# An encoder layer on one core: the 22 stores of the down product's activation forms are issued by GpSimd instead of ScalarE

## The reference

```
h = rmsnorm(x, ffn_norm_g)
gate, up = h @ w_gate_up                     # 512 x 2048 by 2048 x 11264
x = x + (silu(gate) * up) @ w_down           # 512 x 5632 by 5632 x 2048
```

## Time and profile before

| what | value |
|---|---|
| median of 3 runs | 2136.73 us (2135.73 to 2136.99) |
| profiled execution | 2136.44 us, its span in the trace 2134.7 us |
| PE | 2113.3 us busy, 99% of the span |
| DVE | 1526.2 us, 71% |
| ACT | 944.6 us, 44% |
| POOL | 174.2 us, 8% |
| granted TensorE clock | 0.998 of full speed |
| DMA | 376.31 MB, 176 GB/s over the span |

### The profile page before, as it was taken

The page is one execution under the profiler, slowest core; times in us unless marked ns, Lnnn a source line. Parts: engine busy times, 40 slices in busy tenths (PEclk is TensorE's granted clock), DMA queues, the critical chain, the costliest instruction groups (busy, mean ns, idle before and its releaser), DMA issues. The chain is left out here.

```text
span 2134.7 us, 27909 instructions
## 1 busy us (share of the span) xinstructions
PE 2113.3 (99%) x10404; PEld 1845.4 (86%) x10404; DVE 1526.2 (71%) x2108; ACT 944.6 (44%) x1281; POOL 174.2 (8%) x354
## 2 busy tenths in 40 slices
PE   8999999999999999999999999999999999999998
PEld 8999999999998888888888888888888777887876
DVE  4444444444455435888888987987978998999999
ACT  5333333333343335444444444544445554544533
POOL 0322222222221000000000000000000000000000
PEclk9999999999999999999999999999999999999999
DMA  6232333232243344666666666676677877868766
GB/s 185 76 99 79 93 85 92 79 98 79 84 128 128 119 134 132 198 218 200 219 212 211 208 219 212 204 233 204 198 235 232 269 256 246 263 208 269 260 186 203
DMA packets 258924, 376.31 MB, mean 176 GB/s; under 512 B 15842, under 2 KB 114180, under 8 KB 258324
## 3 DMA queue, kind: packets, MB, share of 16 engines
q1 hardware_dynamic: 255456, 354.90, 52.8%
q10 hardware_dynamic: 3380, 20.21, 2.5%
HBM read 346.45 MB, written 28.61 MB: 176 GB/s over the span
## 5 line engine op out<-in xcount | busy, mean ns | idle before, releaser
L1391 DVE TENSOR_TENSOR f_lo<-f_raw,f_hi 128x1536 fp32r<-128x1536 f32 (+1 forms) x230 | 454.4, 1980 | 46.9 <-ACT f_hi L1020 31.4
L564 PE MATMUL gemm<-w_hi,act_t 128*128 128x384 f32 (+2 forms) x1280 | 450.7, 352 | 2.3 <-DVE w_lo L1207 2.3
L565 PE MATMUL gemm<-w_lo,act_t 128*128 128x384 f32 (+2 forms) x1280 | 443.9, 347 | 0.0
L566 PE MATMUL gemm<-w_hi,act_t 128*128 128x384 f32 (+2 forms) x1280 | 443.9, 347 | 0.0
L765 PE MATMUL gemm<-f_hi,a_form 128*128 128x512 f32 x1056 | 411.2, 389 | 0.0
L767 PE MATMUL gemm<-f_hi,a_form 128*128 128x512 f32 x1056 | 411.1, 389 | 0.0
L766 PE MATMUL gemm<-f_lo,a_form 128*128 128x512 f32 x1056 | 410.8, 389 | 0.0
L765 PE MATMUL aux<-f_hi,a_form 128*128 128x512 f32 x792 | 313.2, 395 | 6.7 <-DVE f_lo L1391 5.1
L1207 DVE TENSOR_TENSOR w_lo<-w_raw,w_hi 128x768 fp32r<-128x768 f32 (+1 forms) x160 | 160.7, 1008 | 208.5 <-ACT w_hi L862 208.5
L766 PE MATMUL aux<-f_lo,a_form 128*128 128x512 f32 x792 | 308.5, 390 | 0.0
L767 PE MATMUL aux<-f_hi,a_form 128*128 128x512 f32 x792 | 308.5, 390 | 0.0
(11 more groups left out here) (184 smaller groups left out, 2227.5 us busy)
## 6 DMA issues: line engine op xcount, KB each, us to landing
f_raw<-in_ffn_w_gate_up SPq DMA_DIRECT2D x264, 512.0 KB, 4.2
f_raw<-in_ffn_w_down SPq DMA_DIRECT2D x132, 512.0 KB, 4.8
w_raw<-in_fox_w_in SPq DMA_DIRECT2D x192, 256.0 KB, 3.3
f_raw<-in_ffn_w_gate_up SPq DMA_DIRECT2D x88, 256.0 KB, 4.0
w_raw<-in_fox_w_out SPq DMA_DIRECT2D x16, 1024.0 KB, 5.1
f_raw<-in_ffn_w_down SPq DMA_DIRECT2D x44, 256.0 KB, 4.9
a_raw<-forms_scratch SPq DMA_DIRECT2D x22, 512.0 KB, 6.6
forms_scratch<-fa_a ACTq DMA_DIRECT2D x11, 896.0 KB, 6.3
```

Of the source, the lines that this page charges most:

```text
L564: mm(out, a_hi, b_hi, start=first, stop=False)
L565: mm(out, a_hi, b_lo, start=False, stop=False)
L566: return mm(out, a_lo, b_hi, start=False, stop=last)
L1391: v.tensor_tensor(f_lo[:, n % 4, 0:3 + g], f_raw[:, n % 4, 0:3 + g], f32(f_hi[:, n % 3, 0:3 + g]), ALU.subtract).then_inc(f_lo_done, 1)
```

## The change

The function `store_forms` and its two calls are gone from ACT's program. GpSimd issues the same 22 stores in the same order, each when DVE has signalled the forms of its step, right behind the norm factors and ahead of its two last adds.

```diff
@@ gpsimd
             g.tensor_scalar(rms_neg[:], rms_x[:], -1.0, None, ALU.mult).then_inc(rms2_done, 1)
+
+            for step in range(NSTEP):
+                pool.wait_ge(form_done, 8 + step + 1)
+                pool.dma_start(dram_forms[step], (fa_a, fa_b)[step % 2][:, 0:7])\
+                    .then_inc(forms_stored[step % 2], 16)
@@ scalar
-            def store_forms(r, i):
-                step = 2 * (r - 1) + i
-                act.wait_ge(form_done, 8 + step + 1)
-                act.dma_start(dram_forms[step], (fa_a, fa_b)[i][:, 0:7]).then_inc(forms_stored[i], 16)
-
@@ scalar, first pass
                     if j == 4 and hidden:
                         hidden_forms(r, 1)
-                    if j == 4 and hidden:
-                        store_forms(r, 0)
                 else:
-                    if j == 3 and hidden:
-                        store_forms(r, 1)
```

## The result

The changed kernel takes 2151.5 us (2150.16 to 2154.68, 4 runs) against 2136.86 us for the one before on the same chip: ratio 1.0071, 95% interval 1.0059 to 1.0083. It is 14.6 us slower, outside the range, with the sign and the place that stood in the text as the first rival, at 2143.9 us. The profiled execution took 2151.18 us, its span is 2149.2 us.

What follows compares the result with a forecast made beforehand. TensorE, busy 2113.3 of 2134.7 us, was taken to bound the kernel. 0 (issues) - 2.2 (second pass) + 3.3 (first pass) = +1.1 us on 2136.44 gave 2137.5 us, range 2132.8 to 2143.5.

Steps and rivals of the forecast that it cites:

- the first rival: Slower: fa_b's store shares engines with the second pass's first load every round, 0.7 us each; 2143.9 us, chance 0.26.
- What bounds it: TensorE bounds the kernel; in the SwiGLU half it waits 6.0 us in 10 waits for VectorE's low parts of weights.
- Issues on ScalarE worth nothing: Taking 22 store issues (7 us in all) off ScalarE frees nothing TensorE waits for: value 0.
- The gain in the second pass: Without fa_b's store there, TensorE's waits in rounds 4, 10 and 11 go: -2.2 us, ends 0 and -6.0.
- The limit of 6.4 us: Latest landing after issue of the second pass's first load that costs TensorE nothing, the same in every round.
- where the store stands beside the load: First pass's end: fa_b's store arrives 0.2 to 0.7 us after the load's second half's issue and stands behind it.
- The order of arrival: Transfers run in the order they arrive, read from fa_a's store moving no packet until 932.7 behind earlier loads.
- the price: Delay of the second pass's first load: 0.3 us in 11 rounds, 3.3 us; upper end 7.7 and about 2 more.
- The second, faster: Rival: stores stand behind loads and the first pass hides them; -2.2 to -6.0 us, 2131.9 us, chance 0.10.
- The third, a slow start on GpSimd: Rival: a GpSimd start over 8.3 us makes ScalarE wait for fa_a's memory; at 10 us 2155 us, chance 0.04.

Runs made afterwards that it cites:

- e3: Kernel before, with only the stores of fa_a moved to GpSimd, those of fa_b left on ScalarE at their old place: 2137.36 us, ratio 0.9993.
- f4: Changed kernel, with GpSimd's store of fa_b held until the sums of the second pass's last unit are done: 2132.58 us, ratio 0.9982.
- f2: Kernel before, with ScalarE's store of fa_b two units later in the second pass (j = 5 in place of 3): 2134.45 us, ratio 0.9987.
- g1: Changed kernel, with one unused GpSimd operation of about a microsecond ahead of each store of fa_b: 2141.05 us, ratio 1.0011.
- f1: Changed kernel, with the store of fa_b waiting until the first load of the second pass has landed: 2137.09 us, ratio 1.0005.
- e2: Changed kernel, with GpSimd's store of fa_b waiting for the point in the second pass where ScalarE used to issue it: 2140.12 us, ratio 1.0011.
- e4: Kernel before, with only the stores of fa_b on GpSimd at the changed kernel's time, those of fa_a left on ScalarE: 2155.64 us, ratio 1.0078.
- g2: Changed kernel, with two unused GpSimd operations, 2 us, ahead of each store of fa_b: 2138.42 us, ratio 1.0002.

## Why the prediction was wrong

**What bounds it: right.** The waits of TensorE for low parts are where the change was decided. The sum was misread a little: the earlier trace rows begin at 1230 us, and their 6.0 us leave out the 0.34 of round 4, which the 2.2 us of the gain count; the whole is 6.6 us in 12 waits.

**Issues on ScalarE worth nothing: right.** ScalarE was as busy as before, and e3, which takes half of the issues off it, changed nothing that can be told.

**The gain in the second pass: right in mechanism, somewhat small.** I counted 2.2 us. By the starts of units it is 3.0 in rounds 1 to 10, and the changed kernel has all of it; 3.9 us of the first units, behind their waits and at half clock, stand against it. Moved to a harmless place, the store gives back 3.9 us (f4), 2.0 (f2), by the medians.

**The limit of 6.4 us: right.** Landing less limit is the wait: in round 2, 7.3 - 6.4 = 0.9 us, by the starts of matmuls 0.95; in round 9, 8.6 - 6.4 = 2.2 and 2.2.

**The step that failed: where the store stands beside the load.** I wrote that a store arriving at 934.6 to 935.1 comes "0.2 to 0.7 us after the second half's issue" at 934.4 and "would stand behind it, hurting only the next load". That compares the first packet of one transfer with the issue of another. My estimate for the store, 1 to 1.5 us from the end of the sums, was good: 0.30 us to the issue and 1.10 to the first packet make 1.4, so 934.95. But a second-pass load needs 1.32 us itself, which puts its halves at 935.1 and 935.7. Like compared with like, the store was ahead of both. The order of arrival, which I used against the rival, spoke for it. And I carried over from the earlier trace rows more than they show: there the load came first, and the store waited. With the store first the two went side by side (97 packets and 100 in 3 us), and the load landed after 7.3 us and more in place of 5.5 to 6.4.

**The second error: the price.** I took the one landing of 7.1 us from round 4 for the upper end, 0.7 us a round. It was 7.3 to 7.4 in five rounds (2, 3, 4, 6 and 7) and 7.9 to 8.6 in the other five, so 0.9 to 2.2 us, 1.4 in the mean of ten rounds: 13.9 us for my 3.3, and above my end of 7.7 + 2. A single row could not show that spread. In rounds 1, 5 and 9 the packet of 16 KB named above falls in; what makes rounds 8 and 10 long stays open. I also left out what a wait costs beyond itself: 0.2 us in the unit behind it, and sometimes clock, 3.2 us here.

**The rivals.** The first one was it, with 0.7 for 1.4 us a round. Its number, 2143.9, was still 7.6 us short. The second, faster, fell with the forecast, for the stores didn't stand behind the loads; a gain of its size, 3.9 us, came only where the store was moved out of the way (f4). The third, a slow start on GpSimd, fell: 0.30 us to the issue, no wait at L1083. The Trainium skill (DMA: Bandwidth & Descriptors, Queues, rings and completion order) lets each engine take turns between queues and finish a whole packet of a queue, typically 9 to 17 descriptors, before it switches. I put that aside too soon: in the changed kernel the queues of GpSimd and SyncE did share. But the rule alone does not give both cases. The changed kernel moved about one packet for one, counted as the profile counts them, and g1 moved 437 of the load's, some 27 for each of 16 engines, before the first of the store's. What decides between the two stays open.

## What to carry to other kernels

A transfer that waits for nothing but its data is not free to move: its bytes take time from the load that is issued next to it, so ask of that load how late it may land. Here the 11 stores of `fa_b`, 896 KB each, cost 14.6 us in one place, nothing that can be told in a second (f1), and gave 3.9 us back in a third (f4). Who issued them made no difference that could be told, early or late; at the old place GpSimd's version came out 0.1% slower, just clear of the noise (e2). When the order of two transfers decides, compare first packet with first packet, for a microsecond was worth 12 us.

## What the runs showed of the hardware that I had not expected

- Which transfer comes first decides much, also between GpSimd's queue and SyncE's: with the store's issue 0.5 us ahead of a load's second half or 0.6 us behind it, that half landed after 7.3 or 5.5 us (round 2, changed kernel and g1). Behind the load the store got no turn for 3.0 us; ahead of it, it went alone for half a microsecond and then shared, 97 packets for 100.
- From issue to first packet with nothing else under way: 1.10 us for GpSimd's store of 128 rows of 7168 bytes, 0.83 for ScalarE's (issued at 1045.53 in the kernel before), 1.32 for SyncE's second-pass loads and 1.02 for its first-pass loads. The issue itself took GpSimd 0.53 us and ScalarE 0.33.
- With VectorE busy next to it, as it was at all 11 stores of `fa_a`, no issue of GpSimd's was held up for long: ten took 0.53 us, and the first of all took 0.80.
- The first unit behind a wait of TensorE took 5.63 to 5.66 us in place of 5.44 in the second passes of the changed kernel.
- The granted clock fell to half for 3.4 us at some of TensorE's waits in this half, but not at all of them. Counted by the starts of matmuls, the traces of all runs have eleven waits of 2.0 us or more here; the clock fell at six of them, and at no shorter one. In e4 it fell at two of four that cost 2.2 to 2.8 us, and in g2 not at the longest of all, 3.2 us. Which ones it takes, the runs don't tell.
